# Compressing the samples' cache beside the prompt's sparse attention, in chunks of eight pages

## What is computed

```python
def compress_rows(x, pe, w1, b1, w2):          # keys and values of the cache, per KV group
    segs = x.reshape(b, nseg, 16, g, dh)
    blocks = concatenate([segs[:, j:j + nc] for j in range(2)])   # length 32, stride 16
    flat = (blocks + pe).reshape(b, nc, g, 32 * dh)
    return gelu(flat @ w1 + b1) @ w2
# branch A: attention over the compressed blocks, over the 16 selected blocks of 64 rows,
#           and over a window of 512; gated sum of the three
# branch B: dilated window attention in three groups of 8 heads; branch C: a gating MLP
```

## Time and profile before

| | |
|---|---|
| median of 3 runs | 2266.81 us |
| profiled execution | 2258.88 us, span 2257.2 us |
| TensorE busy | 2016.5 us, 89% of the span |
| TensorE's granted clock over the span | 0.90 of 2.4 GHz |
| block 2 | 201.0 to 437.5 us |
| block 3 | 437.5 to 926 us |
| blocks 4 and 5 | 926 to 1409.4 us |

### The profile page before, as it was taken

The page is one execution under the profiler, slowest core; times in us unless marked ns, Lnnn a source line. Parts: engine busy times, 40 slices in busy tenths (PEclk is TensorE's granted clock), DMA queues, the critical chain, the costliest instruction groups (busy, mean ns, idle before and its releaser), DMA issues. The chain is left out here.

```text
span 2257.2 us, 27140 instructions
## 1 busy us (share of the span) xinstructions
PE 2016.5 (89%) x9306; PEld 1455.8 (64%) x9306; DVE 479.1 (21%) x1227; ACT 338.1 (15%) x850; POOL 278.5 (12%) x508
## 2 busy tenths in 40 slices
PE   6999888898989999699996455999999899999997
PEld 3787655676868676344452121877777688878886
DVE  3401556414050403111412300001110200100001
ACT  3200344303030212111221200000001000000000
POOL 0000000001000000476564630000000000000000
PEclk9995777897979898799997666999999999999999
DMA  9964940284211100577576797422210222212211
GB/s 337 359 233 174 356 167 0 78 313 165 74 39 56 57 0 30 149 224 195 161 221 195 220 319 287 155 75 74 65 56 23 99 66 74 74 65 75 72 49 39
DMA packets 146426, 308.67 MB, mean 137 GB/s; under 512 B 22757, under 2 KB 97832, under 8 KB 143786
## 3 DMA queue, kind: packets, MB, share of 16 engines
q1 hardware_dynamic: 105002, 152.89, 20.4%
q0 software_dynamic: 22912, 146.41, 19.2%
q10 hardware_dynamic: 18432, 8.40, 1.4%
HBM read 296.89 MB, written 102.57 MB: 177 GB/s over the span
## 5 line engine op out<-in xcount | busy, mean ns | idle before, releaser
L1580 PE MATMUL bank<-cx,w 128*128 128x512 f32 x512 | 229.4, 602 | 17.0 <-DMA cx<-in_cmp_pages 17.0
L419 PE MATMUL bank<-hT,wring 128*128 128x272 f32 (+1 forms) x816 | 195.8, 393 | 4.4 <-ACT obT L912 2.7
L422 PE MATMUL bank<-hT,wring 128*128 128x272 f32 (+1 forms) x816 | 195.3, 392 | 0.0
L1580 PEld LDWEIGHTS bank<-cx,w 128*128 128x128 f32 x512 | 96.0, 192 | 136.3 <-issue 136.3
L419 PEld LDWEIGHTS bank<-hT,wring 128*128 128x128 f32 (+1 forms) x816 | 153.2, 188 | 39.2 <-issue 6.5
L422 PEld LDWEIGHTS bank<-hT,wring 128*128 128x128 f32 (+1 forms) x816 | 153.6, 188 | 33.4
L2240 PE MATMUL bank<-aT,wring 128*128 128x272 f32 x512 | 159.2, 393 | 1.7 <-DVE aT L2196 1.7
L2244 PE MATMUL bank<-aT,wring 128*128 128x272 f32 x512 | 159.1, 392 | 0.0
L1565 POOL DMA_DIRECT2D cx<-in_cmp_pages x192 | 104.6, 545 | 439.1 <-issue 430.1
L1341 POOL DMA_DIRECT2D ring<-in_sel_pages x256 | 138.9, 543 | 73.0 <-issue 55.4
L2223 PE MATMUL bank<-hT,wring 128*128 128x272 f32 x512 | 125.0, 398 | 10.7 <-DVE hT L410 10.7
(11 more groups left out here) (294 smaller groups left out, 2211.6 us busy)
## 6 DMA issues: line engine op xcount, KB each, us to landing
wring<-in_w SPq DMA_DIRECT2D x163, 512.0 KB, 3.5
out_new_dil<-in_cache_dil POOLq DMA_DIRECT2D x8, 8176.0 KB, 42.9
ring<-in_sel_pages SPq DMA_DIRECT2D x256, 64.0 KB, 2.7
ring<-in_sel_pages POOLq DMA_DIRECT2D x256, 64.0 KB, 2.5
out_new_dil<-in_cache_dil POOLq DMA_DIRECT2D x8, 2032.0 KB, 12.5
ring<-in_dil_k POOLq DMA_DIRECT2D x14, 1024.0 KB, 7.5
cx<-in_cmp_pages SPq DMA_DIRECT2D x192, 64.0 KB, 3.1
cx<-in_cmp_pages POOLq DMA_DIRECT2D x192, 64.0 KB, 3.5
```

The lines of the kernel that those rows point to most:

```text
L419: pe.matmul(banks[n % 2][0:m, 0:HT], w[:, k * P:k * P + m], hT[:, k, 0:HT], start=(k == 0), stop=(k == KD - 1))
L422: last = pe.matmul(banks[2 + n % 2][0:m, 0:HT], w[:, k * P:k * P + m], hT[:, k, HT:NT], start=(k == 0), stop=(k == KD - 1))
L1580: last = pe.matmul(banks[hf][:, :].rearrange("p (g a s) -> p g a s", g=G, s=8), w1[:, kv, 8 * hf + jj, :], cxh[kv][:, :, :, jj, :].rearran ...
```

## The change

- The samples' compression moves into block 2. A chunk is 8 pages (keys and values, 1 MB, rows of 1 KB), loaded by SyncE alone into one of three buffers that lie in the weight ring; there are 32 chunks. A chunk's product is four parts of 8 products of 128 columns.
- Block 2's loop is written out: 32 attention blocks. Chunks 0 to 3 come before the first scores; chunk n+4 lies in block n, two parts behind the long flips and two behind the values. Scores run one block ahead in place of two, over three banks; the values stay one block behind. GELU and the second projection of a sample follow its four chunks. SyncE loads block 3's nine weight units after the last chunk.
- Blocks 4 and 5 become one block without compression: scores of both groups (selected and dilated keys by turns), then values of both groups (selected and dilated values by turns), 72 quads in all through the same ring of four. Transfers of 1 MB alternate between the two queues in pairs. The two groups' scores have buffers of their own (`T[gg]`).
- The page table is loaded and clamped in block 1. GpSimd's four bulk copies stay at the start of block 2.

```diff
+        def load_chunk(sp, c):
+            b, q = c // 4, c % 4
+            if c >= 3:
+                sp.wait_ge(s_x, c - 2)
+            for i, page in enumerate(page_numbers(mybir.EngineType.SP, b * PAGES + 8 * q, 8)):
+                sp.dma_start(cxb[c % 3][:, 256 * i:256 * i + 256],
+                             t["cmp_pages"][bass.ds(page, 1), :, :].rearrange("o p n -> (o p) n")
+                             ).then_inc(s_xl[c % 3], 16)
+
+        def chunk_pe(pe, c, part):
+            kv, hf = part // 2, part % 2
+            if part == 0:
+                pe.wait_ge(s_xl[c % 3], 128 * (c // 3 + 1))
+                if c >= 2:
+                    pe.wait_ge(s_xa, c - 1)
+            x = cxb[c % 3].rearrange("p (a v g j s) -> p a v g j s", a=8, v=2, g=G, j=JJ)
+            for jj in range(JJ):
+                last = pe.matmul(
+                    banks[5 + c % 2][:, P * part:P * part + P].rearrange(
+                        "p (g a s) -> p g a s", g=G, s=8),
+                    w1[:, kv, 8 * hf + jj, :],
+                    x[:, :, kv, :, jj, :].rearrange("p a g s -> p g a s"),
+                    start=(jj == 0), stop=(jj == JJ - 1))
+            if part == 3:
+                last.then_inc(s_x, 1)
...
             @block.sync
             def _(sp):
-
+                for c in range(CHUNKS):
+                    load_chunk(sp, c)
+                sp.wait_ge(s_x, CHUNKS)
                 load_units(sp, wr, U_DIL, RING)
...
+                hidden_pe(pe, cxp, nsegp, 0, 0)
+                chunk(0)
+                hidden_pe(pe, cxp, nsegp, 1, 0)
+                chunk(1)
+                chunk(2)
                 second_pe(pe, nsegp, hidp, 0)
+                chunk(3)
                 pe.wait_ge(s_ckr, 1)
-                with pe.Fori(0, R) as r:
...
+                scores_pe(pe, 0)
+                for n in range(NBLOCKS):
+                    c = n + AHEAD
+                    more = c < CHUNKS
+                    if n + 1 < NBLOCKS:
+                        scores_pe(pe, n + 1)
+                    flip_long_pe(pe, n)
+                    if more:
+                        chunk_pe(pe, c, 0)
+                        chunk_pe(pe, c, 1)
+                    flip_short_pe(pe, n)
+                    if n:
+                        values_block_pe(pe, n - 1)
+                    if more:
+                        chunk_pe(pe, c, 2)
+                        chunk_pe(pe, c, 3)
+                    if n % 4 == 3:
+                        project_pe(pe, n // 4, min(n + 2, NBLOCKS))
+                values_block_pe(pe, NBLOCKS - 1)
...
         for gg in range(2):
             QUADS += [("win_k", gg, 0)]
             for c in range(9):
-                QUADS += [("dil_k", 0, c)] if gg else []
+                QUADS += [("dil_k", gg, c)]
                 QUADS += [("sel", gg, c)] if c < 8 else []
-            QUADS += [("sel_v", gg, c) for c in range(8)] + [("win_v", gg, 0)]
-        QUADS += [("dil_k", 1, n) for n in range(9)]
-        QUADS += [("dil_v", gg, n) for gg in range(2) for n in range(9)]
+        for gg in range(2):
+            for c in range(9):
+                QUADS += [("sel_v", gg, c) if c < 8 else ("win_v", gg, 0), ("dil_v", gg, c)]
...
-            return (1, 0) if n % 2 == 0 else (0, 1)
+            return (1, 0) if n % 4 < 2 else (0, 1)
```

More of the change, by code:

```diff
@@ L991, in trunk @@
         vcP = sb("vcP", [NC_P, P], p2)
[L992 to L996, removed]
+        hid = sb("hid", [HID, 2, 2, G, NSEG], p2)
+        hsq = sb("hsq", [HID, G, NSEG], p2)
+        CHUNKS = 4 * B
+        AHEAD = 4
+        NBLOCKS = R * NBLK
+        cxb = [wr[:, 2 * i:2 * i + 2, :].rearrange("p u n -> p (u n)") for i in range(3)]
+        s_xl = [sem(f"chunk_landed{i}") for i in range(3)]
@@ new lines, in chunk_act @@
+        def chunk_act(act, c):
+            b, q = c // 4, c % 4
+            act.wait_ge(s_x, c + 1)
+            if q == 0 and b >= 2:
+                act.wait_ge(s_h2, b - 1)
+            for kv in range(2):
+                last = act.activation(
+                    hid[:, b % 2, kv, :, 64 * q:64 * q + 64],
+                    banks[5 + c % 2][:, 256 * kv:256 * kv + P].rearrange("p (g s) -> p g s", g=G),
+                    ACT.Identity, bias=bias[:, kv:kv + 1])
+            last.then_inc(s_xe, 1)
@@ new lines, in outer_unit_dve, with project_pe @@
+        def outer_unit_dve(dve, b, kv):
+            h = hid[:, b % 2, kv, :, 0:NC_S]
+            dve.wait_ge(s_ht, 2 * b + kv + 1)
+            dve.scalar_tensor_tensor(out=h, in0=hsq[:, :, 0:NC_S], scalar=1.0, in1=h, op0=ALU.add,
+                                     op1=ALU.mult).then_inc(s_ho, 1)
+        def project_pe(pe, b, read):
+            pe.wait_ge(s_ho, 2 * b + 2)
+            pe.wait_ge(s_sread, read)
+            h = hid[:, b % 2]
+            for g in range(G):
+                pe.matmul(banks[7][g * DH:g * DH + DH, 0:NC_S], w2[:, 0, :], h[:, 0, g, 0:NC_S],
+                          start=True, stop=True)
+            for c, m in enumerate((P, NC_S - P)):
+                for g in range(G):
+                    at = 256 + c * P + g * DH
+                    last = pe.matmul(banks[7][0:m, at:at + DH], h[:, 1, g, c * P:c * P + m],
+                                     w2[:, 1, :], start=True, stop=True)
+            last.then_inc(s_h2, 1)
@@ new lines, in flip_long_pe, with flip_short_pe @@
+        def flip_long_pe(pe, n):
+            r, hh, r0, i, w = place(n)
+            pe.wait_ge(s_prob, n + 1)
+            if n:
+                pe.wait_ge(s_ptc, 3 * n)
+            for bank, off in ((2, 0), (3, w)):
+                for kt in range(i + 1):
+                    last = pe.transpose(banks[bank][:, kt * P:kt * P + P],
+                                        att_T[n % PBUF][:, off + kt * P:off + kt * P + P], ident)
+                last.then_inc(s_tp, 1)
+        def flip_short_pe(pe, n):
+            r, hh, r0, i, w = place(n)
+            pe.wait_ge(s_ptc, 3 * n + 1)
+            pe.transpose(banks[2][0:NC_P, 0:P], att_T[n % PBUF][:, 2 * w:2 * w + NC_P],
+                         ident).then_inc(s_tp, 1)
@@ new lines, in values_block_pe @@
+        def values_block_pe(pe, n):
+            r, hh, r0, i, w = place(n)
+            if n % NBLK == 0:
+                pe.wait_ge(s_att, r + 1)
+            pe.wait_ge(s_ptc, 3 * n + 3)
+            pT = att_pT[n % 2]
+            o = banks[4][r0:r0 + DH, i * P:i * P + P]
+            for kv in range(2):
+                for kt in range(i + 1):
+                    pe.matmul(o, v_nat[:, kv, kt, r0:r0 + DH],
+                              pT[:, 512 * kv + kt * P:512 * kv + kt * P + P],
+                              start=(kv == 0 and kt == 0), stop=False)
+            pe.matmul(o, vcP[:, r0:r0 + DH], pT[0:NC_P, 1024:1024 + P], start=False,
+                      stop=True).then_inc(s_pv, 1)
@@ L1400, in sel_act @@
             act.wait_ge(s_s, 8 * gg + c + 1)
-            act.activation(T[:, 512 * c:512 * c + 512], banks[4 + c % 2][:, :],
+            act.activation(T[gg][:, 512 * c:512 * c + 512], banks[4 + c % 2][:, :],
                            ACT.Copy).then_inc(s_sr, 1)
[L1404 to L1411, removed]
@@ new lines, in flip_act @@
+        def flip_act(act, gg, k):
+            at = 10 * gg + k
+            act.wait_ge(s_ft, at + 1)
+            if at >= 3:
+                act.wait_ge(s_e, at - 2)
+            bank, to = banks[4 + at % 3], pT[:, at % 3, :]
+            if k < 9:
+                act.activation(to, bank[:, :], ACT.Copy).then_inc(s_fc, 1)
+                return
+            for i, (c0, m) in enumerate(turns_of(k)):
+                last = act.activation(to[0:m, P * i:P * i + P], bank[0:m, P * i:P * i + P], ACT.Copy)
+            last.then_inc(s_fc, 1)
@@ new lines, in values_pe @@
+        def values_pe(pe, gg, k):
+            at = 10 * gg + k
+            pe.wait_ge(s_fc, at + 1)
+            if k == 0:
+                pe.wait_ge(s_wr, 2)
+                if gg:
+                    pe.wait_ge(s_om, gg)
+            if k < 9:
+                n = QAT[("sel_v", gg, k) if k < 8 else ("win_v", gg, 0)]
+                quad_landed(pe, n)
+            else:
+                pe.wait_ge(s_vn, 32)
+            for i, (c0, m) in enumerate(turns_of(k)):
+                for j in range(GB):
+                    b = GB * gg + j
+                    if k < 9:
+                        v = ring[:, n % NQ, j, P * i:P * i + P]
+                    else:
+                        v = (vc[:, b, 0, :], vc[0:m, b, 1, :], vnew[:, b, :])[i]
+                    last = pe.matmul(banks[7][NS * j:NS * j + NS, 0:P],
+                                     pT[0:m, at % 3, P * i + NS * j:P * i + NS * j + NS], v,
+                                     start=(k == 0 and i == 0), stop=(k == 9 and i == 2))
+            last.then_inc(s_e, 1)
```

968 lines of the change are left out of this document (462 added, 506 removed).

## The result

The changed kernel takes 2287.7 us (median of 4 runs, 2284.5 to 2289.7) against 2265.4 us before on the same chip: ratio 1.0097, 95% interval 1.0077 to 1.0116. It is slower by 1%, as forecast. The profiled execution took 2284.5 us, its span 2282.8.

The account below looks back on a forecast made before the run. Block 2's loop was taken as TensorE-bound, its start as held by bulk copies, the sample block as transfer-bound. Cost 258 less gain 232 gave +26 us on the median of 2266.8: 2293 us, range 2245 to 2335.

Parts of the forecast that it names:

- The collision at the start: Block 2's start: chunk pages wait for GpSimd's bulk copies, about 75 us of the block's 258 us cost.
- the earlier trace: Profile before, 215 to 245 us: 161 large packets of q0 against 160 of q1, one for one whatever their size.
- One step: Block 2's start: four of chunk 0's eight pages get through before the first large packets, at about 205 us.
- the 18 forecast for a pair: Block 2's start: about 18 page packets pass per engine while a pair of bulk copies runs, one in about 3 us.
- The loop: Block 2: TensorE bounds it without waits at full clock, 11.7 us a block, 328 us for 28 blocks with a chunk.
- Rival 2: Block 2's loop does not keep its clock: at 0.85 a block takes 13.8 us, +58 us, 2350 us; chance 0.12.
- The last four blocks: Block 2's end: blocks without a chunk run at the chain's pace, 27 us, with 2 us more to the block's end.
- The sample block: Old blocks 4 and 5: 251 us in place of 483.4, bounded by transfers, a gain of 232 us.
- Its two terms: Sample block: 75.5 MB streamed at 323 GB/s, 234 us, plus about 2, 4 and 11 us at start, middle and end.
- Rival 3: Sample block streams slower than 323 GB/s: 285 us in place of 251, kernel 2327 us; chance 0.15.
- Rival 1: Block 2's start: pages not held one for one, a chunk takes 24 us, kernel 2249 us; chance 0.13.
- Sum: Whole kernel: 258 us cost less 232 us gain, +26 us on the profiled 2258.9; 2293 us against the median 2266.8.

Follow-up runs that it names:

- e1: The changed kernel with block 2's four GpSimd bulk copies moved to block 3: 2209.0 us, ratio 0.9725 to the kernel before.
- e2: The changed kernel with block 2's four bulk copies left out altogether: 2207.5 us, ratio 0.9728 to the kernel before.
- e3: The changed kernel with block 2's four bulk copies at the same place, written in rows of 3.5 KB: 2260.1 us, ratio 0.998 to the kernel before.
- e5: e1 with a block's values directly behind its own short flip instead of one block later: 2239.9 us, ratio 0.9851 to the kernel before.
- e6: e1 with all four parts of a chunk behind the values, none before the short flip: 2226.0 us, ratio 0.978 to the kernel before.
- e9: e1 with the sample block's whole quads dealt to the two queues by turns, not two and two: 2203.4 us, ratio 0.9742 to the kernel before.
- e12: e9's kernel run once more, side by side with a repeat of e1 on one chip: 2206.0 us, ratio 0.9726 to the kernel before.
- e7: The changed kernel with block 2's four bulk copies put into its loop, one at a time: 2240.6 us, ratio 0.9864 to the kernel before.

## Why the prediction was right

**The collision at the start (about 75 us).** Right in size and cause. The wait is 75.9 us; the earlier trace rows carried over from 4 KB to 1 KB, and e1, e2 and e3 show from three sides that it is the copies. First scores were forecast at 333 and came at 336.6. One step was wrong: half of chunk 0, 36 packets an engine, was to pass before the first large packets. SyncE's first request went out at 202.8, behind GpSimd's copies at 202.3, and until 205 no packet of q1 passed. From 202 to 254 us, all of the first pair's time:

```profile
q0 software_dynamic: 277, 16.74, 95.1%
q1 hardware_dynamic: 308, 0.29, 2.4%
```

That is 308 / 16 = 19 an engine, the 18 forecast for a pair, and the 36 are missing. Between the pairs, from 254 to 260 us:

```profile
q1 hardware_dynamic: 1631, 1.48, 78.0%
q0 software_dynamic: 24, 0.85, 37.6%
```

1631 / 16 = 102, somewhat under the forecast's 115 to 125. It would have been enough for the 18 + 72 packets that the forecast had left of chunks 0 and 1, but 53 + 72 were left. So chunk 1 missed the gap and TensorE found chunks 1 and 2 ready together at 312.8: it did both behind the copies, and the first scores came 3.6 us later than forecast. The error stayed this small because the end of the second pair decides, and that was right (near 312.5 for 313).

**The loop.** Forecast 11.7 us a block, measured 320.1 / 28 = 11.43. A chunk takes 3.57 + 3.77 = 7.34 us by the starts of the next pieces (forecast 7.2), the rest 4.1 instead of 4.5. TensorE bounds it without a wait; e5 and e6 show that each of the two covers is needed for that (25 and 17 us of block 2). Rival 2 (clock 0.85) is refuted by the 0.99.

**The last four blocks.** 32 us instead of 29: TensorE waits for VectorE 0.8, 1.7 and 3.4 us.

Together: 342.3 instead of 339, 320 instead of 328, 32 instead of 29, end at 694.4 instead of 696. Errors of 3 to 8 us cancelled; the cost of 256 for 258 owes something to that.

**The sample block.** Forecast 251, measured 252.4 us, gain 231 for 232. Its two terms were each off: the stream ran at 310 to 314 GB/s, not 323, which adds 8 us to 234, and what does not overlap with it was 10 us, not 17. Over eleven more profiles without a change of its work, or with the other dealing, it took 248 to 260, so a hit within 2 us owes something to luck. Rival 3 (285 us) is refuted.

**Rival 1** (a page's descriptors pass as one packet, 2249 us) is refuted by 168 packets of 1 KB for 168 large ones, and by the time: it had chunk 0 landed at 217, and TensorE got it at 258.7. The Trainium skill ("DMA: Bandwidth & Descriptors", the section on queues, rings and completion order) has an engine drain a packet of typically 9 to 17 descriptors at a time; in this kernel q1 passes one row per turn at 1, 2 and 4 KB, so the measurement decides against it here. The queue that GpSimd fills did put two rows into a packet in e3.

**Sum.** +26 forecast on the profiled execution, 2284.5 - 2258.9 = +25.6 measured; by medians of one chip +22.3. The 2293 lay 5 us high: 4 us are the +22.3 for +26, and 1 us is that the median of before was 2265.4 in these runs and not 2266.8.

Open: why e9's and e12's sample blocks differ by 11 us was not traced. All copies were on GpSimd's queue and all pages on SyncE's; whether another pair of queues takes turns in the same way was not run.

## What to carry to other kernels

Before work that waits for small-row transfers is moved, look at which large copies are in flight there, and count packets, not bytes: here, with the copies on GpSimd's queue and the rows on SyncE's, each engine passed one small row per large packet while they lasted. Place such copies where nothing is wanted sooner than they take, or cut them until one piece is shorter than the lead of the buffers. When TensorE bounds a loop, put its independent work in front of each step that waits for a copy, half here and half there: the two places were worth 25 and 17 us of block 2.

## What the runs showed that was not expected

- A copy written in rows of 3.5 KB went in packets of 6.8 KB at 0.30 us, about 23 GB/s an engine, against 21 for packets of 59 KB at 2.8 us. The copies got little slower by it (the first pair ended 59 us after its start instead of 54), while the transfers beside them went eight times as fast.
- A wait of 5 to 6 us in a loop that ran at the upper clock cost about 2 us more behind it, while the clock came back (e7: 21.5 us of waits, 8.4 us of longer products).
